# A hybrid DeltaNet / RG-LRU layer on one core: back-substitution and query sums in four column groups, and ScalarE's work in the scan in another order

## The reference

```python
a_mat = jnp.where(strict, jnp.einsum('bhnik,bhnjk->bhnij', kb, k) * decay, 0.0)
lower = a_mat + jnp.eye(CHUNK, dtype=f32)
sol = lax.linalg.triangular_solve(lower, rhs, left_side=True, lower=True, unit_diagonal=True)
u, w = sol[..., :dv], sol[..., dv:]
...
def step(s, xs):
    w_c, u_c, qg_c, qk_c, kd_c, dl_c = xs
    v_new = u_c - jnp.einsum('bhck,bhkv->bhcv', w_c, s)
    o_c = jnp.einsum('bhck,bhkv->bhcv', qg_c, s) + jnp.einsum('bhcj,bhjv->bhcv', qk_c, v_new)
    s = s * dl_c[..., None, None] + jnp.einsum('bhck,bhcv->bhkv', kd_c, v_new)
    return s, o_c
```

## Time and profile before

| | us |
|---|---|
| median of 3 runs (1557.0 to 1558.54) | 1557.43 |
| the profiled execution | 1558.14 |
| its span | 1556.3 |
| PE busy in it | 1523.4 (98%) |
| DVE busy | 1012.8 (65%) |
| ACT busy | 793.1 (51%) |
| POOL busy | 360.4 (23%) |

### The profile page before, as it was taken

How to read it: one execution, slowest core, us unless ns; L and a number is a source line. 1 busy time by engine, 2 the same in 40 slices (tenths; PEclk the granted TensorE clock), 3 DMA queues, 4 the chain that set the end, 5 groups by cost and what they waited for, 6 DMA issues and landing times.

```text
span 1556.3 us, 26570 instructions
## 1 busy us (share of the span) xinstructions
PE 1523.4 (98%) x10680; PEld 1436.6 (92%) x10680; DVE 1012.8 (65%) x1766; ACT 793.1 (51%) x1627; POOL 360.4 (23%) x297
## 2 busy tenths in 40 slices
PE   8999999999999999999999999999999999999997
PEld 3699999999999999999689999999999999999886
DVE  2679888797978888897853767357447631423444
ACT  5265665847565665847338636636645620311211
POOL 2221323222221323222201222122112211242111
PEclk9999999999999999999999999999999999999999
DMA  9221222130221212131421211212112451444123
GB/s 321 75 65 28 76 60 76 32 104 20 63 69 46 76 53 83 32 104 32 137 66 50 78 57 59 69 56 78 53 54 78 134 177 42 131 141 141 41 82 135
DMA packets 116005, 127.37 MB, mean 82 GB/s; under 512 B 6477, under 2 KB 97446, under 8 KB 115882
## 3 DMA queue, kind: packets, MB, share of 16 engines
q1 hardware_dynamic: 115594, 125.34, 25.5%
q10 hardware_dynamic: 288, 0.33, 0.1%
HBM read 105.56 MB, written 20.09 MB: 81 GB/s over the span
## 4 chain that ended last, share of the span: by engine, by line
PE 77%; DVE 11%; ACT 4%; DMA 4%; issue 3%; SPq 0%; POOL 0%; DVEq 0%; POOLq 0%; ACTq 0%
PE mb L124 15%; PE mb L126 14%; PE mb L125 14%; PE db L124 6%; PE db L126 6%; PE db L125 6%; DVE d_qg L1407 3%; DVE d_qg L1405 2%; PE db L1151 2%; PE db L1123 2%; PE db L1167 2%; PE db L1161 1%; PE db L1140 1%; PE db L880 1%; PE db L1074 1%
## 5 line engine op out<-in xcount | busy, mean ns | idle before, releaser
L124 PE MATMUL mb<-h_hi,w_hi 128*128 128x384 f32 x1088 | 363.9, 334 | 1.6 <-POOL w_lo L1752 0.9
L125 PE MATMUL mb<-h_lo,w_hi 128*128 128x384 f32 x1088 | 363.5, 334 | 0.0
L126 PE MATMUL mb<-h_hi,w_lo 128*128 128x384 f32 x1088 | 363.5, 334 | 0.0
L124 PE MATMUL db<-h_hi,w_hi 128*128 128x384 f32 x808 | 284.5, 352 | 2.0 <-ACT d_row L564 2.0
L126 PE MATMUL db<-h_hi,w_lo 128*128 128x384 f32 x808 | 271.4, 336 | 0.5 <-issue 0.5
L125 PE MATMUL db<-h_lo,w_hi 128*128 128x384 f32 x808 | 271.4, 336 | 0.0
L1752 POOL TENSOR_TENSOR w_lo<-w,w_hi 128x1024 fp32r<-128x1024 f32 x47 | 128.3, 2731 | 466.0 <-ACT w_hi L1781 466.0
L124 PEld LDWEIGHTS mb<-h_hi,w_hi 128*128 128x128 f32 x1088 | 204.2, 188 | 2.5 <-POOL w_lo L1752 1.2
L125 PEld LDWEIGHTS mb<-h_lo,w_hi 128*128 128x128 f32 x1088 | 204.2, 188 | 0.0
L126 PEld LDWEIGHTS mb<-h_hi,w_lo 128*128 128x128 f32 x1088 | 204.2, 188 | 0.0
L124 PEld LDWEIGHTS db<-h_hi,w_hi 128*128 128x128 f32 x808 | 152.6, 189 | 5.7 <-issue 2.9
(11 more groups left out here) (311 smaller groups left out, 2945.3 us busy)
## 6 DMA issues: line engine op xcount, KB each, us to landing
w<-in_w_in SPq DMA_DIRECT2D x48, 512.0 KB, 4.1
d_dt<-decay_rows SPq DMA_DIRECT2D x16, 576.0 KB, 6.3
d_qg<-decay_rows SPq DMA_DIRECT2D x16, 512.0 KB, 4.2
w<-in_w_gate SPq DMA_DIRECT2D x16, 512.0 KB, 4.1
branch_a<-d_kq SPq DMA_DIRECT2D x8, 576.0 KB, 3.2
branch_b<-l_z SPq DMA_DIRECT2D x8, 576.0 KB, 2.8
merge_gates_b<-l_gates SPq DMA_DIRECT2D x8, 576.0 KB, 5.4
m_in<-merge_gates_b SPq DMA_DIRECT2D x8, 576.0 KB
```

The lines of the kernel that those rows point to most:

```text
L124: pe.matmul(out, hi, rhi, start=(k == 0), stop=False)
L125: pe.matmul(out, hi, rlo, start=False, stop=False)
L126: return pe.matmul(out, lo, rhi, start=False, stop=(last and stop))
```

## The change

Four things. The query sums take 36 matmuls with weights of 32 columns in place of 9 with 128 (one per tile and column group). Levels 2 and 3 of the back-substitution take their two parts in turns, and part 1 writes to other partitions (`back_at`), so that four column groups take part; the copies read there and take part 1 first. ScalarE's work in the scan stands in another order, with the value silu in two halves (`silu_value`). The filling is dealt out by one table, `shares`; and in the last head the four LRU taps stand ahead of the scan on VectorE.

```diff
+        def back_at(level, d, p):
+            return (back_row(level, d) + p * (2 if level == 3 else 1 if d else 3) * B) % P
...
+            def silu_value(h, half):
+                cs = (slice(0, HALF_ROW), slice(HALF_ROW, CONV))[half]
+                act.wait_ge(S["taps"], order(h, 1) + 1)
+                ins = act.activation(v2[:, cs], v2[:, cs], ACT.Silu)
+                if half:
+                    ins.then_inc(S["silu"], 1)
...
-                    for p, (t0, t1) in enumerate(back_parts(level)):
+                    for p, (t0, t1) in reversed(tuple(enumerate(back_parts(level)))):
...
-                        high(X1 if last else block_of(h + 1, 0))
                         act.wait_ge(S["ov"], (h * STEPS + 1) * DIRS)
                         act.activation(kacc[:, 0, :], bank[0][:, 0:P], ACT.Copy).then_inc(S["o0"], 1)
+                    if s == (0 if last else 4):
+                        high(X1 if last else block_of(h + 1, 0))
                     if not last:
-                        if s == 1:
+                        if s == 0:
                             first_tap(h + 1, 2)
-                        elif s == 2:
+                        elif s == 1:
                             silu(h + 1, 0)
                         elif s == 7:
-                            silu(h + 1, 1)
-                        for n in range(*((0, 0), (0, 0), (0, 0), (0, 2), (2, 7), (7, 13), (13, NI), (0, 0), (0, 0))[s]):
+                            silu_value(h + 1, 0)
+                        elif s == 8:
+                            silu_value(h + 1, 1)
+                        for n in range(*((0, 0), (0, 0), (0, 2), (2, 7), (7, 8), (8, 14), (14, NI), (0, 0), (0, 0))[s]):
                             decays(h + 1, n)
...
                 for t in range(NT):
-                    mm = pe.matmul(bank[2][:, 3 * P + t:3 * P + t + 1], cb_[:, tile_at(t):tile_at(t) + P], ones,
-                                   start=True, stop=True)
+                    for b in range(Q):
+                        mm = pe.matmul(bank[2][b * B:(b + 1) * B, 3 * P + t:3 * P + t + 1],
+                                       cb_[:, tile_at(t) + b * B:tile_at(t) + (b + 1) * B], ones, start=True, stop=True)
...
+                shares = (0, 8, 2, 2, 1, 1, 1, 1, 2, 1, 1, 2, 1, 1) if last else (2, 2, 2, 3, 1, 3, 2, 2, 2, 1, 1, 1, 1, 1)
...
-                    for p, (t0, t1) in enumerate(back_parts(level)):
-                        for t in range(t0, t1):
+                    parts = back_parts(level)
+                    for i in range(max(t1 - t0 for t0, t1 in parts)):
+                        for p, (t0, t1) in enumerate(parts):
+                            if t0 + i >= t1:
+                                continue
                             for d in range(DIRS):
...
-                per_step = (2, 2, 2, 2, 2, 2, 1, 1, 1) if not last else (1, 1, 1, 2, 1, 1, 2, 1, 1)
...
+                else:
+                    for a in range(TAPS):
+                        lru_tap(a)
...
-                    if last and 1 <= s <= TAPS:
-                        lru_tap(s - 1)
```

More of the change, by code:

```diff
@@ L1040, in front_tensor, with fill @@
                         mm.then_inc(S["gl_mm"], 1)
-                tiles = 5 if last else 1
-                if not last:
-                    project(block_of(h, 3), 0, range(0, 1))
+                units = [(g, k) for g in range(NG) for k in range(KT)]
+                shares = (0, 8, 2, 2, 1, 1, 1, 1, 2, 1, 1, 2, 1, 1) if last else (2, 2, 2, 3, 1, 3, 2, 2, 2, 1, 1, 1, 1, 1)
+                def fill(n):
+                    first = sum(shares[:n])
+                    for g, k in units[first:first + shares[n]]:
+                        project(block_of(h, 3), g, (k,))
+                fill(0)
                 pe.wait_ge(S["uz"], (h + 1) * Q)
@@ L1067, in back @@
                     width = level * B
-                    for p, (t0, t1) in enumerate(back_parts(level)):
-                        for t in range(t0, t1):
+                    parts = back_parts(level)
[3 more added lines that the diff above has]
+                                continue
                             for d in range(DIRS):
-                                row0 = back_row(level, d)
+                                t, row0, at = t0 + i, back_row(level, d), back_at(level, d, p)
                                 col = (4 - level) * B if d == 0 else 0
                                 ks = slice(0, P) if level == 3 else (slice(P // 2, P), slice(0, P // 2))[d]
-                                mm = pe.matmul(back_bank(level, d, p)[row0:row0 + B, (t - t0) * width:(t - t0 + 1) * width],
+                                mm = pe.matmul(back_bank(level, d, p)[at:at + B, i * width:(i + 1) * width],
                                                umat[ks, t, row0:row0 + B], vinv(d, t)[ks, col:col + width],
@@ L1078, in back @@
                                     mm.then_inc(S["it"], 1)
-                between = (0, range(0, KT)) if last else (0, range(1, 3))
-                after_1 = (1, range(0, 2)) if last else (0, range(3, 5))
-                after_2 = (1, range(2, 4)) if last else (0, range(5, KT))
-                after_3 = (1, range(4, 5)) if last else (1, range(0, 1))
-                def bridge(g, ks):
-                    project(block_of(h, 3), g, ks)
                 if last:
                     pe.wait_ge(S["gl_row"], 2)
-                bridge(*between)
+                fill(1)
                 pe.wait_ge(S["mt_out"], (h + 1) * NG)
@@ L1107, in front_tensor @@
                 back(3)
-                bridge(*after_3)
-                units = [(g, k) for g in range(1, NG) for k in range(KT)][tiles:]
-                per_step = (2, 2, 2, 2, 2, 2, 1, 1, 1) if not last else (1, 1, 1, 2, 1, 1, 2, 1, 1)
-                def fill(s):
-                    first = sum(per_step[:s])
-                    for g, k in units[first:first + per_step[s]]:
-                        project(block_of(h, 3), g, (k,))
+                fill(4)
                 def outputs(s):
@@ L1451, in front_vector @@
                 scaled_query(1)
[L1452 to L1454 removed]
+                for p, (t0, t1) in reversed(tuple(enumerate(back_parts(3)))):
+                    row0, at, width = back_row(3, 1), back_at(3, 1, p), 3 * B
+                    dve.wait_ge(S["it"], h * 10 + 6 + (2 - p) * DIRS)
                     dve.tensor_copy(w2[row0:row0 + B, NT + t0:NT + t1, 0:width],
[L1456 removed]
+                                    back_bank(3, 1, p)[at:at + B, 0:(t1 - t0) * width].rearrange(
                                         "p (t c) -> p t c", c=width)).then_inc(S["it_dve"], 1)
```

19 lines of the change are left out of this document (8 added, 11 removed).

## The result

The changed kernel takes 1539.21 us (median of 4 runs, 1538.48 to 1540.62), the kernel before in the same comparison 1557.51 (1557.0 to 1558.54). The ratio is 0.9883, 95% interval 0.9866 to 0.9900: faster by 18.3 us, where 13.8 was forecast. The profiled execution took 1538.48 us with a span of 1536.7 (before 1558.14 and 1556.3), at the same granted clock of 0.997.

What follows compares the result with a forecast made beforehand. TensorE's work plus waits for `vnu` and `vn` was taken as the bound from the inverse to scan end. Heads 0 to 6 gave 11.0 us, the last 2.8: 1557.4 - 13.8 = 1543.6, forecast 1541 to 1546.5, range 1538 to 1551.

Steps and rivals of the forecast that it cites:

- What bounds: Up to M, the start of the inverse, the VectorE chain; from there to scan end TensorE's work plus waits.
- Query sums: Ahead of the inverse: 72 narrow records take 1.35 us instead of 1.93, saving 0.58 a head as room for filling.
- Levels: Back-substitution levels 2 and 3: four groups save 0.41 and 0.64 us; copies let the first p2 come only 0.52 sooner.
- Steps 0 and 1: Start of the scan: added unit and `vnu` behind value taps leave 1.6 us gained in heads 0 to 6.
- High part: Scan, heads 4 to 6: `high` in step 4 removes waits from GpSimd's subtraction meeting step 1's value tap, 2.7 us.
- Rival 3: Step 4 of the scan: `w_lo` starts ahead of the value tap and holds it, 12 us, giving 1556; 5%.
- Steps 4 and 5: Scan: one filling unit less each gains 1.06 us, late `vnu` loses 0.52, leaving 0.54 a head.
- End of the scan: Halving the value silu lets the last `vn` come in time within 0.05 us, gaining 0.42 a head.
- Rival 1: Sums and levels: records can't follow sooner than 25 ns, 5 us less gain, giving 1548.6; 10%.
- Rival 2: Levels: four groups stream no faster than two, 6 to 7 us less gain, about 1550.5; 7%.
- rival 4: Query sums: a 32-column load costs 107 ns like a 128-column one, sums take 7.7 us, about 1587; 4%.
- Rival 5: Charged waits (first p2, steps 4 and 5) are smaller, 5 us more gain, giving 1539; 12%.

Runs made afterwards that it cites:

- experiment 1: Changed kernel with levels 2 and 3 back in two column groups, part 0 whole, then part 1, copies in the old order: 1542.56 us, ratio to before 0.9912.
- Experiment 9: Changed kernel with one filling unit of heads 0 to 6 moved from step 0 to behind level 3: 1536.08 us, ratio to before 0.9865.
- Experiment 3: Changed kernel with ScalarE making the high part of the next weights in step 0 of the scan again: 1543.55 us, ratio to before 0.9924.
- experiment 6: Changed kernel with the last head's four LRU taps back in steps 1 to 4 of its scan: 1540.38 us, ratio to before 0.9901.
- experiment 5: Changed kernel with the 36 narrow query sums ordered one column group after the other: 1546.87 us, ratio to before 0.9936.
- experiment 10: Changed kernel with one filling unit moved from step 0 to behind level 3 and one from step 3 to ahead of the inverse: 1534.57 us, ratio 0.9853.

## Why the prediction was near, point by point

The gain was 18.3 us and not 13.8. Most of the mechanism came as forecast; two terms were mis-sized, the query sums and, with more effect, steps 0 and 1.

**What bounds.** Right. From the transposes to M the time is the same to 0.1 us in heads 1 to 6, whatever TensorE had saved there; the 0.56 of experiment 1 comes from the copies. From M of head 3 to that of head 4 it is 85.30 us, where about 86.1 was forecast.

**Query sums.** The term was mis-sized: 1.35 us forecast, 0.71 measured. The step that failed is "since the rows of L1060 have the very shape of these weights": those matmuls move 32 to 128 columns and the sums one, so the 17.7 ns were a pace of theirs and not of their loads. How much of it the columns take was not tested. My lower bound, 14 ns a record, was no bound either. It moved the total little, since what was saved stood ahead of M as idle time: 0.23 was forecast, 0.7 to 0.8 came out. With what the sums save net, 1.10, the forecast's own sum gives it: 0.18 - 0.53 + 1.10 = 0.75. That it gave room and not time was foreseen, how much room was not.

**Levels.** 0.72 and 0.97 forecast, 0.68 and 0.95 measured. Copies of level 3 at 0.94, measured 0.92 and 0.96. First p2 0.52 sooner; 0.56 measured, 3.9 us in seven heads (the 3.06 and 4.67 of the table hold a stall of this kernel or of the kernel before). The wait of 0.5 us came with 0.57. I had named VectorE's copy as its cause; the profile charges ScalarE's, which ends at 425.35, while VectorE's ends at 425.57, 0.11 ahead of the p2, which the program lets wait for both. It is VectorE's: in every head of every trace the first p2 starts 0.09 to 0.11 behind the end of VectorE's copy, while its distance from ScalarE's is 0.22 to 0.23 in the kernel before and 0.32 to 0.33 here.

**Steps 0 and 1** is the term that was furthest off: I let 2.04 of the 3.64 be lost again, and 0.12 was. I had the p2 of step 1 wait for `vnu` in heads 0 to 3, behind taps that run beside the select. In the changed kernel the distance is 4.75 and 4.71 in heads 1 and 3, which is TensorE's own work without a wait (5.34 and 5.28 in heads 0 and 2, with one), and the taps of head 3 took 2.50 instead of 2.81, since the select begins later against M: 12.58 us behind it, before 11.79. I had let the taps move towards a select that stands still, and it doesn't stand still: in the two executions of the changed kernel the heads that wait are those in which it begins 11.7 to 11.8 us behind M, heads 0 and 2 in the first and 0 and 5 in the second, and where it begins at 12.1 or later none waits. The other side: heads 4 to 6 went from 4.37, 4.54 and 4.53 up to 4.72, 4.74 and 4.72, the price of the added unit, 0.19 to 0.35 a head. Experiment 9 shows a better place for the unit.

**High part.** 2.7 forecast, 3.76 measured: the waits of heads 4 to 6 went as said (4.82, 4.45 and 4.45 to 3.39), which is 3.55 of it. I had priced them by the idle time that the profile charges, 1.1 + 0.8 + 0.8, and the distances shrank by 1.43, 1.06 and 1.06. Experiment 3 shows that undoing it now costs more than it had saved. Rival 3, `w_lo` ahead of the tap of step 4, did not come: in head 3 the tap starts at 442.16, the subtraction at 442.74, 0.58 behind it, with 0.6 forecast, and in all seven heads the tap keeps its 0.81. By the Trainium skill, "SBUF — State Buffer", section "Terms", the port that VectorE and GpSimd share is locked for a whole instruction; the tap of 1.87 in experiment 3, which ends only behind the subtraction, agrees with it.

**Steps 4 and 5.** 3.78 forecast, 4.18 measured (less 0.60 a head). The distances from p2 of 3, 4 and 5 to the next went from 3.39, 3.39, 2.87 to 3.01, 3.11, 2.97. With a unit at 0.52 that is 0.14, 0.24 and 0.10 lost, 0.48 in all, where I had charged 0.26 twice.

**End of the scan.** 0.42 a head forecast, 0.48 measured. **Last head:** 2.54 and 2.56; experiment 6 confirms it alone.

**Rivals.** Rival 1 (no start nearer than 25 ns) falls with 9.8 ns. The Trainium skill, "TensorE: Matmul & The Clock Gate", section "Wait — 56ns, not 53.3ns?", gives that distance; within one column group experiment 5 shows 28.7 ns, near to it, and over four groups the 9.8 ns contradict it. Rival 2 falls with the paces of the levels, rival 4 with the sums. Rival 5 gave 1539, and 1539.2 came out, but that is luck and not its mechanism: of the waits that it names the one ahead of the first p2 was longer than charged (0.57 for 0.5), and steps 4 and 5 gave only 0.4 us more. The extra gain came from places that it doesn't name: 1.9 us in steps 0 and 1, 1.1 from the high part, 0.4 at the end of the scan and some 0.8 between the transposes and M, nearly all of it in the last head, where TensorE waits for weights by DMA.

## What to carry to other kernels

Small matmuls with 32 weight columns gain by following each other in different column groups: what counts is whether the next matmul goes to another group, more than how small each is. When work disappears ahead of a point that another engine sets, look at once for idle time there and behind the next copies, and move filling into both: here that was some 2.5 to 2.8 us more by the pieces (experiment 10), with nothing but a table of shares changed. A cost from a collision on a port should be recomputed for the new starts of both parties, since small shifts decide how often they meet: in three heads before, in six in experiment 3 and in none in the changed kernel.

## What the runs showed of the hardware

- Loads of 32 columns with one moving column: 9.8 ns a record over four column groups in turn, 28.7 ns in one group; with 128 weight columns 107 ns.
- A level of 36 records with 96 moving columns: 0.95 us over four groups in turns, 1.32 over four in two parts, 1.61 over two. One group starts a record every 82 to 83 ns in all of them (55 to 56 with 64 columns).
- Going over from matmuls with 128 weight columns to the narrow sums cost 0.10 us in the products ahead (2.10 for 2.00).
- After 2.07 us of one-column matmuls in one group after another the granted clock fell to 1.2 GHz for 3.4 us in four of eight heads, though TensorE was not idle by the trace; after 1.93 us of wide ones or 0.71 of the short ones it did not.
- A VectorE tap of 0.81 us took 1.87 beside a GpSimd subtraction of 2.37 and ended 0.62 behind it.
- A stall of TensorE of 1.0 to 1.4 us, charged to issue, inside the inverse, in some executions of a kernel and not in others. It goes with a late transfer of 16 KB of instructions (0.8 to 1.5 us behind M in place of 4.0 ahead of it); that this is its cause was not tested.
